# A decoder trunk with PEER experts: gather steps spread anew over the blocks, first weight tiles loaded one block earlier

## The reference

```python
# per layer: rms norm -> one input projection, whose columns feed (A) a Mamba-2 SSD mixer and
# (B) sparse attention; both are projected, gated, summed, projected out and added to x;
# then rms norm -> PEER experts -> added to x
def peer(h, p):
    n = h.shape[0]
    q = (h @ p['peer_wq']).reshape(n, PEER_HEADS, 2, PEER_HALF)
    s = jnp.einsum('nhcd,chkd->nhck', q, p['peer_keys'], preferred_element_type=F32)
    s1, i1 = lax.top_k(s[:, :, 0], PEER_TOPK)
    s2, i2 = lax.top_k(s[:, :, 1], PEER_TOPK)
    ...
    g = jax.nn.softmax(top_s, axis=-1)
    act = jax.nn.gelu(jnp.einsum('nd,nhkd->nhk', h, p['peer_u'][eidx], preferred_element_type=F32))
    return jnp.einsum('nhk,nhkd->nd', (g * act).astype(h.dtype), p['peer_v'][eidx])
```

## Time and profile before

| | |
|---|---|
| median of three runs | 1571.76 us (1567.11 to 1576.45) |
| the profiled execution, its own time | 1571.38 us |
| its span, first to last instruction | 1569.8 us |
| mean granted TensorE clock | 0.842 |
| TensorE, VectorE, ScalarE, GpSimd busy | 71%, 55%, 35%, 23% |
| moved by DMA | 418.81 MB, mean 267 GB/s |
| of it through GpSimd's queue (gathers, some cache pages) | 278.94 MB |

### The profile page before, as it was taken

The page is one execution under the profiler, slowest core; times in us unless marked ns, Lnnn a source line. Parts: engine busy times, 40 slices in busy tenths (PEclk is TensorE's granted clock), DMA queues, the critical chain, the costliest instruction groups (busy, mean ns, idle before and its releaser), DMA issues. The chain is left out here.

```text
span 1569.8 us, 21163 instructions
## 1 busy us (share of the span) xinstructions
PE 1108.1 (71%) x6844; PEld 721.8 (46%) x6844; DVE 866.8 (55%) x2415; ACT 554.9 (35%) x1577; POOL 362.7 (23%) x447
## 2 busy tenths in 40 slices
PE   5968999998869876747655447579598455555554
PEld 4846678887749773324222115377375111111110
DVE  1025369993153126739756447655355566676763
ACT  1135225565250024846444207421233223323322
POOL 1331001210000011312221221112333344444552
PEclk8978999999799997968876768789799787788877
DMA  4543234444018485969999973779899999999996
GB/s 157 169 127 108 68 107 124 137 130 148 14 46 311 171 306 178 337 251 352 376 362 348 356 287 137 266 309 383 352 371 392 373 412 413 406 413 407 414 403 256
DMA packets 90713, 418.81 MB, mean 267 GB/s; under 512 B 12336, under 2 KB 33344, under 8 KB 52080
## 3 DMA queue, kind: packets, MB, share of 16 engines
q0 software_dynamic: 40096, 278.94, 44.9%
q1 hardware_dynamic: 49408, 137.01, 25.3%
q10 hardware_dynamic: 1104, 1.56, 0.3%
HBM read 405.73 MB, written 11.59 MB: 266 GB/s over the span
## 5 line engine op out<-in xcount | busy, mean ns | idle before, releaser
L1686 POOL DMA_INDIRECT pe_uv<-d_uv,pe_idx x256 | 289.6, 1131 | 882.4 <-PE pe_acc L1767 627.1
L1767 PE MATMUL pe_acc<-pe_uv,pe_dg 64*64 64x512 f32 x2048 | 322.0, 756 | 188.7 <-ACT pe_dg L1739 188.7
L1702 DVE CUSTOM_DVE_ANT_0 pe_uv<-pe_uv,pe_hnat 128x1024 f32<-128x1024 f32 x256 | 308.8, 1223 | 179.9 <-DMA pe_uv<-d_uv,pe_idx 179.8
L183 PE MATMUL pi_ps<-xn,pi_w 128*128 128x264 f32 x1104 | 263.3, 399 | 12.9 <-PEq L88 12.5
L1767 PEld LDWEIGHTS pe_acc<-pe_uv,pe_dg 64*64 64x64 f32 x2048 | 78.3, 158 | 382.9 <-ACT pe_dg L1739 289.9
L183 PEld LDWEIGHTS pi_ps<-xn,pi_w 128*128 128x128 f32 x1104 | 216.1, 198 | 53.1 <-issue 15.0
L1723 ACT ACTIVATE pe_gl<-pe_a 128x2 f32<-128x2 f32 x132 | 26.6, 202 | 369.8 <-DVE pe_a L1702 369.5
L1953 PE MATMUL pq_ps<-pq_hN,pq_w 128*128 128x128 f32 (+1 forms) x512 | 70.5, 298 | 26.7 <-DMA pq_w<-d_wq 26.6
L1953 PEld LDWEIGHTS pq_ps<-pq_hN,pq_w 128*128 128x128 f32 x512 | 66.1, 207 | 37.0 <-DMA pq_w<-d_wq 28.9
L1739 ACT ACTIVATE pe_dg<-cst,pe_w 128x64 f32<-128x64 f32 x256 | 73.1, 332 | 0.0
L1733 ACT ACTIVATE pe_w<-pe_gl,pe_gw 128x1 f32<-128x1 f32 x256 | 61.4, 287 | 5.2
(11 more groups left out here) (307 smaller groups left out, 1620.0 us busy)
## 6 DMA issues: line engine op xcount, KB each, us to landing
pi_w<-d_w_in SPq DMA_DIRECT2D x81, 512.0 KB, 3.6
mg_w<-d_w_ab SPq DMA_DIRECT2D x16, 1536.0 KB, 7.4
pq_w<-d_wq SPq DMA_DIRECT2D x32, 512.0 KB, 8.8
mg_wo<-d_w_out SPq DMA_DIRECT2D x16, 512.0 KB, 8.8
as_kv<-d_ck SPq DMA_DIRECT2D x64, 128.0 KB, 13.2
ss_h<-d_state SPq DMA_DIRECT2D x8, 1024.0 KB, 6.1
o_ssm_s<-ss_h SPq DMA_DIRECT2D x8, 1024.0 KB, 12.7
as_kv<-d_cv SPq DMA_DIRECT2D x64, 128.0 KB, 6.6
```

The costliest lines, as they stand in the source:

```text
L183: mm = pe.matmul(self.ps[:, n % BANKS, 0:T], self.w[:, n % WSLOTS, c * P:(c + 1) * P], self.k.xn[:, c, :], start=c == 0, stop=c == KD - 1)
L1686: pool.indirect_dma_start(self.uv[:, u % self.RING, :], None, self.k.d_uv[:], bass.IndirectOffsetOnAxis(ap=src, axis=0)).then_inc(self.gat ...
L1702: dve.tensor_tensor_reduce(self.uv[:, r, 0:D_MODEL], self.uv[:, r, 0:D_MODEL], h[:], 1.0, 0.0, ALU.mult, ALU.add, self.a[:, p % self.PAIRS ...
L1767: mm = pe.matmul(self.acc[half * HD:(half + 1) * HD, q, :], self.dg[rows, r, :], self.uv[rows, r, vals], start=False, stop=False, skip_gro ...
```

## The change

1. `ends` becomes `[0, 5, 20, 35, 47, 58, 64]`: five pairs in `queries(0)` (in slots 9 to 15), 15 in `attend_prompt(1)` (12 before), 15 in `attend_sample` (24), 12 in `ssd_chunk(1)` (7), 11 in `merge(1)` (11), 6 in `queries(1)` (10). The rest stays 68 pairs.
2. `hankel[1]` is loaded in `queries(0)`, behind the keys and before query tile 4.
3. The first two `w` tiles of `merge` and `gn` are loaded in `ssd_chunk` (`mw.first`); `merge` has two `w` slots in place of three.
4. The first four query tiles and `g2` are loaded in `merge` (`qw.first`), issued after the last `w` tile and before the first `wo` tile.
5. To make room: `lm`, `em` and `mx` share three buffers, `ea` is gone, `pq` has four buffers in `queries(0)`, `merged` of part 1 lies in `hT`.

```diff
@@ ssd_chunk
-        xdt, xdec, bnat, cb, lm, em, mx, ea, ce = tensors(
+        xdt, xdec, bnat, cb, mx = tensors(
...
-                if g >= 2:
-                    act.wait_ge(mixed, g - 1)
                 for r in range(4):
-                    e = act.activation(em[:, g % 2, r, :], lm[:, g % 2, r, :], ACT.Exp, bias=heads(k.nac, 4 * g + r, 1))
+                    e = act.activation(mx[:, g % 3, r, :], mx[:, g % 3, r, :], ACT.Exp, bias=heads(k.nac, 4 * g + r, 1))
...
-                if g >= 2:
-                    dve.wait_ge(em_ready, g - 1)
-                dve.tensor_tensor(lm[:, g % 2], pl[:, g % 2], k.negt.unsqueeze(1).broadcast_to([P, 4, P]), ALU.add
+                if g >= 3:
+
+                    dve.wait_ge(y_done, g - 2)
+                dve.tensor_tensor(mx[:, g % 3], pl[:, g % 2], k.negt.unsqueeze(1).broadcast_to([P, 4, P]), ALU.add
...
-        if c:
-            @block.sync
-            def _(sp):
+        @block.sync
+        def _(sp):
+            mw.first(sp)
+            if c:
                 sp.wait_ge(h_out, GROUPS)
@@ merge
+class MergeWeights:
+
+    SLOTS = 2
...
+    def first(self, sp):
+
+        for n in range(self.SLOTS):
+            self.load(sp, n)
+        sp.dma_start(self.gn[:], self.k.d_gssd[:]).then_inc(self.g_loaded, 16)
+
+
+class QueryWeights:
...
+    def first(self, sp):
+
+        sp.dma_start(self.g2[:], self.k.d_g2[:]).then_inc(self.g_loaded, 16)
+        for n in range(WSLOTS):
+            self.load(sp, n)
...
-            sp.dma_start(gn[:], k.d_gssd[:]).then_inc(g_loaded, 16)
-            for n in range(KD):
-                if n >= SLOTS:
-                    sp.wait_ge(multiplied, n - SLOTS + 1)
-                sp.dma_start(w[:, n % SLOTS, :], k.d_w_ab[n]).then_inc(w_loaded[n % SLOTS], 16)
+            for n in range(SLOTS, KD):
+                sp.wait_ge(multiplied, n - SLOTS + 1)
+                mw.load(sp, n)
+            qw.first(sp)
             for n in range(KD):
                 if n >= 4:
                     sp.wait_ge(out_done, n - 3)
@@ queries
+        RQ = NT if last else 4
...
-        at = shares(pairs, NT)
+        at = shares(pairs, NT) if last else [[]] * 9 + shares(pairs, NT - 9)
...
-            for n in range(NT):
-                if n >= WSLOTS:
-                    sp.wait_ge(multiplied, n - WSLOTS + 1)
-                sp.dma_start(w[:, n % WSLOTS, :], k.d_wq[n]).then_inc(w_loaded[n % WSLOTS], 16)
-                if n == 0:
-                    sp.dma_start(keys[:], k.d_keys[:]).then_inc(k_loaded, 16)
+            sp.dma_start(keys[:], k.d_keys[:]).then_inc(k_loaded, 16)
+            if not last:
+                hankel = bass.AP(tensor=k.s_table.tensor, offset=0, ap=[[1, P], [BIAS_N, HEADS], [1, TP]])
+                sp.dma_start(k.hankel[1][:], hankel).then_inc(k.hankel_loaded, 16)
+            for n in range(WSLOTS, NT):
+                sp.wait_ge(multiplied, n - WSLOTS + 1)
+                qw.load(sp, n)
...
                 ex.weights(dve, 0)
+                for p in pairs:
+                    ex.dots(dve, p)
                 return
@@ build
-    ends = [0, 12, 36, 43, 54, 64]
+    ends = [0, 5, 20, 35, 47, 58, 64]
```

More of the change, by code:

```diff
@@ L906, in _, with ssd_chunk @@
                 k.proj.multiply(pe, n)
-def ssd_chunk(nc, k, c, ex=None, pairs=()):
+def ssd_chunk(nc, k, c, mw, ex=None, pairs=()):
     xbc, zs, Y, rms = k.xbc[c], k.zs[c], k.Y[c], k.rms[c]
@@ L1894, in move, with queries @@
         sp.wait_ge(self.moved, 64)
-def queries(nc, k, ex, part, pairs):
+def queries(nc, k, ex, part, qw, pairs):
     NT, PSB, H_AT = 2 * PH, 2, 4
@@ L1964, in _ @@
             scores(PH - 1)
+            for m in (NT, NT + 1):
+                for p in late(at, m, 2):
+                    ex.mix(pe, p)
             if last:
-                for m in (NT, NT + 1):
-                    for p in late(at, m, 2):
-                        ex.mix(pe, p)
                 pe.wait_ge(widened, 1)
@@ L1996, in _ @@
                 act.wait_ge(multiplied, n + 1)
-                act.activation(pq[:, n, :], qps[:, n % PSB, 0:W], ACT.Copy).then_inc(evacuated, 1)
+                if n >= RQ and n % 2 == 0:
+                    act.wait_ge(keyed, (n - RQ) // 2 + 1)
+                act.activation(pq[:, n % RQ, :], qps[:, n % PSB, 0:W], ACT.Copy).then_inc(evacuated, 1)
                 if n % 2 == 0 and n:
@@ L2007, in _ @@
             scores(PH - 1)
+            for p in late(at, NT, 1):
+                ex.weigh(act, p)
             if last:
-                for p in late(at, NT, 1):
-                    ex.weigh(act, p)
                 act.wait_ge(keyed, PH + 1)
@@ L2088, in attend @@
         k.Y[0], k.rms[0] = tensors(nc, early, "right", Y0=(P, KI, P), rms0=(P, GROUPS, P))
-        ssd_chunk(nc, k, 0)
-        merge(nc, k, 0)
+        mw = MergeWeights(nc, early, k, 0, "right")
+        ssd_chunk(nc, k, 0, mw)
+        qw = QueryWeights(nc, ctx, k, 0, "left")
+        merge(nc, k, 0, mw, qw)
+    return qw
 def build(nc, ins, outs):
@@ L2129, in build @@
                     k.att, k.vnat, k.negp = tensors(nc, prompt, att=(P, N_ATT, T), vnat=(P, 2, 2 * P), negp=(P, 2, TP))
-                    attend(nc, k, prompt)
-                    ex = Experts(nc, last, k)
-                    queries(nc, k, ex, 0, [])
-                    k.hankel[1], = tensors(nc, prompt, hankel1=(P, HEADS, TP))
-                    attend_prompt(nc, k, 1, [], ex, pairs[0])
-                attend_sample(nc, k, ex, pairs[1])
+                    k.hankel_loaded = signals(nc, prompt)("hankel")
+                    with ExitStack() as query:
+                        qw = attend(nc, k, query)
+                        ex = Experts(nc, last, k)
+                        k.hankel[1], = tensors(nc, prompt, "right", hankel1=(P, HEADS, TP))
+                        queries(nc, k, ex, 0, qw, pairs[0])
+                    attend_prompt(nc, k, 1, [], ex, pairs[1])
+                attend_sample(nc, k, ex, pairs[2])
             k.Y[1], k.rms[1] = tensors(nc, trunk, Y1=(P, KI, W), rms1=(P, GROUPS, W))
-            ssd_chunk(nc, k, 1, ex, pairs[2])
-            merge(nc, k, 1, ex, pairs[3])
+            mw = MergeWeights(nc, trunk, k, 1, "left")
+            ssd_chunk(nc, k, 1, mw, ex, pairs[3])
+            qw = QueryWeights(nc, last, k, 1, "right")
+            merge(nc, k, 1, mw, qw, ex, pairs[4])
         with last:
             ex.more(nc, last)
-            queries(nc, k, ex, 1, pairs[4])
+            queries(nc, k, ex, 1, qw, pairs[5])
 OUTS = dict(o_conv_p=(P, KC, 3), o_conv_s=(P, KC, TS, 3), o_k=(P, 2, T), o_v=(P, 2, T), o_ik=(HD, T),
```

74 lines of the change are left out of this document (45 added, 29 removed).

## The result

| | before | after |
|---|---|---|
| median | 1573.28 us (4 runs, 1567.11 to 1576.45) | 1620.18 us (4 runs, 1610.62 to 1628.89) |
| ratio, 95% interval | | 1.0302 [1.0234, 1.0369] |
| profiled execution's span | 1569.8 us | 1608.9 us |
| granted clock | 0.842 | 0.823 |

The change makes the kernel 3.0% slower. The forecast was 1579, its range ended at 1602. The spans of the two profiled executions differ by 39.1 us, the medians by 46.9: the profiled execution of after is the fastest of its four.

A forecast was written before the change was run, and what follows sets the result against it. Transfers were taken to bound the last block, queries(1) and attend_sample, latency the blocks receiving pairs. Terms 4 + 15 + 6 - 40 + 30 + 8 - 17 + 2 = +8 on 1571.38 gave 1579 us; range 1545 to 1602.

The forecast's parts named there:

- closes: Across blocks: five more contexts clear semaphores and add a barrier, four on the path: +2 us, bounds 0 and +4.
- three such turns +24, the first double slot +3.5: ssd_chunk(1): rounds of the three-pair gather ring take 23 us for 14.8, +24; first slot with two pairs +3.5.
- one pair more in the tail +2.5: ssd_chunk(1): one more pair falls in the block's tail, +2.5 us.
- PE's 3 us of idling behind hankel: queries(0): keys and 2048 KB of hankel stand ahead of query tile 4 on SP's queue, so PE idles some 3 us.
- the stall of tile 2: merge(0): w tile 2, issued only after product 0, lands at 486.3, so PE waits 3.3 us.
- 0.77 more: merge(0): with two w slots each later step takes 6.13 us, 0.77 more, some 3.5 over the rest.
- just make it: merge(0): without gathers, the wo tiles land just in time.
- Rival C: Merges: two w slots stall at every tile, +8 and +15 us, total 1590; chance 0.07.
- the prediction's rival B: attend_sample: keeps its pace, set by SP's stores and DVE's updates, -20 in place of -40, total 1599; chance 0.14.
- the prediction's rival D: attend_sample: mixed traffic is dearer than the last block's, 5.94 us a pair, nine are -53, total 1566; chance 0.06.
- Rival A: Whole kernel: the gather ring doesn't bind, gathers run in idle DMA time, -37 us, total 1534; chance 0.25.
- the sum of the upper bounds: Whole kernel: all terms at their upper bounds together, left out of the range 1545 to 1602.

The follow-up runs named there:

- Run 4: The changed kernel, but ssd_chunk(1) issues no gathers for merge(1), which issues its first six itself: 1607.71 us, ratio 1.0238 to the kernel before.
- run 1: The changed kernel with five pairs of ssd_chunk(1) given back to attend_sample (7 and 20 pairs): 1597.09 us, ratio 1.0168 to the kernel before.
- run 2: The kernel before with only the spread changed, to 12, 23, 12, 11, 6 pairs, so twelve in ssd_chunk(1): 1611.86 us, ratio 1.0254.
- run 3: The changed kernel with the spread of the kernel before, no pair in queries(0): 1578.12 us, ratio 1.0054 to the kernel before.
- Run 8: Run 7 with two w slots in place of three in both merges: 1590.79 us, ratio 1.0107 to the kernel before.
- run 11: Kernel before plus hankel in queries(0), query tiles behind the last wo tile, six wo tiles in w slots, no gathers for merge(1) from ssd_chunk(1): 1562.64 us, ratio 0.9948.
- run 5: The changed kernel, but PE mixes the pairs of ssd_chunk(1) one slot after their dots instead of two: 1610.05 us, ratio 1.0244 to the kernel before.
- run 12: Like run 11, but ssd_chunk(1) gathers ahead again and five pairs move from attend_sample to queries(0): 1569.86 us, ratio 0.9986 to the kernel before.
- run 7: The changed kernel with the spread of before, merge and queries loading their own first tiles, three w slots: 1572.18 us, ratio 1.0002 to the kernel before.

## Why the prediction was wrong

The direction was right for every block, and the blocks that gain came within 3 us of the forecast. The sum failed on one term above all.

| term | forecast | measured |
|---|---|---|
| merge(0) | +4 (-2.5 to +8) | +8.7 |
| queries(0) | +15 (+5 to +25) | +24.9 |
| attend_prompt(1) | +6 (-2 to +14) | +7.0 |
| attend_sample | -40 (-47 to -20) | -37.4 |
| ssd_chunk(1) | +30 (+17 to +34) | +48.4 |
| merge(1) | +8 (-4 to +15) | +7.3 |
| queries(1), whole block | -17 (-22 to -8) | -14.2 |
| closes | +2 | inside the lengths above |
| blocks up to merge(0) | 0 | -5.6 |

**ssd_chunk(1), the step that failed.** The turns were near: up to the last `mx` the block grew from 66.0 to 98.8 us, +32.8 where "three such turns +24, the first double slot +3.5" make 27.5. What failed is "one pair more in the tail +2.5". From the last `mx` to the end are 33.3 us where 17.7 stood, +15.6. Of that, 9.7 lie before the end of the last mix and 5.9 in the drain (9.73 us before, 15.66 now). The 9.7 are 5.7 of products (7.65 us for three pairs, 1.95 for one) and 4.0 ahead of them, where DVE now does the dots of the last slot. The count itself was wrong: with twelve pairs over eight slots three are mixed behind the last work where one was, so two more and not one. And the forecast left the drain at its 9 us, where it is the landing of all that was just issued, now six gathers in 8.3 us. Run 4 shows that the whole drain is idle time, by taking it away (-13.3 us), runs 1 and 2 that the pairs are the cause and the buffers are not. The shared buffers did cost nothing, as forecast (82.2 us in run 3, 83.7 before).

**queries(0).** The choice came 3.0 us earlier within the block (10.8 after its start, before 13.8), not 4. The first gather took 11.4 us to its dots, not 9, with query tiles on the wires beside it; the first mix ended 5 us later than forecast and the last gather went out 64.7 us after the block's start, not 58.3. Then came 12.2 us of drain for 9. Each of these is a few us, and all point the same way. The +25 that was written as the bound is what happened. PE's 3 us of idling behind hankel are not there: its waits for query tiles in this block come to 2.6 us in all.

**merge(0).** The head gave 1.7 of 2.5, and the stall of tile 2 was 2.7 of 3.3. The later steps took more than "0.77 more" each (8.6 us over six steps, the stall of tile 2 among them): 5.7 of waits for `w`, and 1.8 since the 48 products behind the long one ran at a lower clock (2.98 and 4.48 us for 1.95 and 3.74); and the `wo` tiles did not "just make it" (1.9 us). Rival C had the sum of this merge (+8) and its stalls at nearly every tile (five of six), though four of the five are short, 3.0 us together; in `merge(1)`, where it said +15, PE waits three times, 4.0 us in all. Run 8 gives the whole price of the missing slot, 10 us a merge.

**attend_prompt(1), attend_sample, merge(1), queries(1)** came within 3 us, in part by luck. Hankel was worth 7.3 us (run 3), not 10, and three pairs more 14.3, not 16, so that two errors cancel. They cancel in `merge(1)` too: its first gating comes 1.4 us earlier in the block (forecast 2), from there to the eighth are 6.2 more (forecast 4), and behind it 2.5 more (forecast 6). The five waits of SP for state stores shrank from 37.8 to 28.2 us, neither kept (the prediction's rival B) nor gone. `merge(1)` waited once for `mg_wo`, as forecast, but 3.5 us and not 6. On the prediction's rival D (5.94 a pair) the sample block says 4.2 a pair over the nine that left it; that is a mean of 2.2 for the first four and 5.7 for the next five (run 1), so the forecast's 4.4 was near as a mean and was no price of a pair. The page "DMA: Bandwidth & Descriptors" of the Trainium skill (section "Where 436 GB/s comes from") has the HBM side bind at some 358 GB/s a core. The trace disagrees again, with 397 GB/s over the 121.8 us of `merge(1)` in run 11. (The prediction counts five slices at 412 to 414 GB/s in the earlier trace rows; there are four, which changes nothing.)

**The blocks ahead of the change** were 5.6 us shorter in the profiled execution of after. More than half of it is in `time_steps`, which took 39.8 us before, 36.7 after, 36.6 in run 5, and 39.8 again in runs 1 and 3, whose code is the same there. So it is scatter, and a part of why the medians lie further apart than the spans.

**Rival A** had a quarter of the chance. It said that low DMA shares mean free time for gathers. Runs 2 and 12 close it: idle wires in a block whose engines take turns don't take in gathers, since each gather waits for a mix.

**The range** ended at 1602 since "the sum of the upper bounds" was left out. The chunk's upper bound of +34 was itself too low by 14. Chunk and `queries(0)` missed on the same side, and in part for one reason, drains longer than the 9 us of an emptier block (15.7 and 12.2), so that their errors added up.

## What to carry to other kernels

Before work is moved into a block that looks idle, count per slot: where a prefetch ring of n items meets slots that consume them at nearly n per turn, each item costs its part of the whole round trip (8.7 us in the chunk here, 5.3 in the last block, where transfers bound), whatever the DMA share says. And don't take a block's price from one step: the same block gave back 2.2 us a pair for the first four and 5.7 for the next five. Look at what is left behind the last work of a block: a barrier waits for every gather issued, so issues in a burst at the end are idle time, unless the next block would wait for the same bytes anyway. And a third buffer on a stream whose loads last longer than one step was worth more here than an early start (10.2 us against 1.9 in `merge(0)`): compare the load's landing with one step, not with the block's head.

## What the runs showed of the hardware

- A block whose POOL issued gathers ends only when they have landed: 15.7 us from the last mix to the next block with six outstanding, 1.0 us with none (run 4). In run 4 the first gather of `merge(1)` shows 27.50 us of waiting on POOL's own queue: it had nothing left to issue and stood at the barrier.
- Behind a stall of 2.72 us PE ran at half clock for a while: granted 0.50 from 482.5 to 484.2, and 16 products in 2.98 us for 1.95. In run 7 a wait of 5.21 us (556.67) was followed by 16 in 3.79.
- The same edit can be pure gain or nothing: holding back six gathers gave 13.3 us for 1.3 in the change (run 4), and 11.3 for 7.9 in run 11, where `merge(1)` then ran at 397 GB/s.
